# Two token-wise products inside block 2's attention: the copy out of PSUM moves from ScalarE to VectorE

## The reference, cut to what matters

```python
h = rms_norm(x, norm_g)
proj = jnp.einsum('btd,de->bte', h, w_in)
a_q, a_k, a_v, a_g, b_q, b_k, b_v, b_g, m_q, m_g = jnp.split(proj, cuts, axis=-1)
...
oa = from_heads(moba_attention(qa, ka, to_heads(a_v, 6)))       # heads "a", 6 of 64
ob = from_heads(dilated_attention(qb, kb, to_heads(b_v, 6)))    # heads "b", 6 of 64
om = from_heads(memory_attention(qm, km, to_heads(m_v, 4)))     # memory heads, 4 of 64
y = jnp.concatenate([oa * silu(a_g), ob * silu(b_g), om * silu(m_g)], axis=-1)
return x + jnp.einsum('bte,ed->btd', y, w_out)
```

## Time and profile before

| | |
|---|---|
| median of 3 runs | 1651.87 us (1651.77 to 1654.35) |
| the profiled execution's own time | 1654.05 us |
| its span | 1652.2 us |
| TensorE busy | 1583.6 us, 96% |
| VectorE busy | 912.7 us, 55% |
| ScalarE busy | 770.0 us, 47% |
| mean granted TensorE clock | 0.997 |

### The profile page before, as it was taken

How to read it: one execution, slowest core, us unless ns; L and a number is a source line. 1 busy time by engine, 2 the same in 40 slices (tenths; PEclk the granted TensorE clock), 3 DMA queues, 4 the chain that set the end, 5 groups by cost and what they waited for, 6 DMA issues and landing times.

```text
span 1652.2 us, 22035 instructions
## 1 busy us (share of the span) xinstructions
PE 1583.6 (96%) x8345; PEld 1307.0 (79%) x8345; DVE 912.7 (55%) x1924; ACT 770.0 (47%) x1599; POOL 46.7 (3%) x75
## 2 busy tenths in 40 slices
PE   6999999999999999999999999999999999989999
PEld 6887768788887887777788888898866679977667
DVE  4597546443445379546444335568664464965443
ACT  4443444333334352545333334435667553456772
POOL 0000001000001000001100000100000010000000
PEclk9999999999999999999999999999999999999999
DMA  7232112333332333112233333332212233311121
GB/s 217 87 89 77 51 39 77 92 100 90 90 106 75 98 102 90 52 52 79 65 89 102 99 92 115 99 90 69 70 37 62 75 90 96 96 45 58 40 76 64
DMA packets 80885, 136.07 MB, mean 82 GB/s; under 512 B 8190, under 2 KB 33548, under 8 KB 80780
## 3 DMA queue, kind: packets, MB, share of 16 engines
q1 hardware_dynamic: 77120, 129.22, 26.9%
q10 hardware_dynamic: 3660, 5.44, 1.2%
HBM read 132.55 MB, written 2.10 MB: 81 GB/s over the span
## 4 chain that ended last, share of the span: by engine, by line
PE 82%; DVE 8%; ACT 7%; issue 2%; DMA 0%; ACTq 0%; POOL 0%; DVEq 0%
PE gemm_bank L725 68%; PE aux_bank L851 3%; PE aux_bank L830 2%; PE aux_bank L795 2%; PE aux_bank L811 2%; ACT probs L1160 2%; PE aux_bank L780 1%; DVE w_lo L1466 1%; ACT w_hi L1104 1%; PE aux_bank L839 1%; ACT spread_inv L1174 1%; ACT probsT L1195 1%; DVE rope L1565 1%; DVE probs L1624 1%; PE aux_bank L697 1%
## 5 line engine op out<-in xcount | busy, mean ns | idle before, releaser
L1104 ACT ACTIVATE w_hi<-raw 128x512 fp32r<-128x512 f32 (+3 forms) x524 | 305.1, 587 | 640.9 <-PE gemm_bank L725 640.3
L1466 DVE TENSOR_TENSOR w_lo<-raw,w_hi 128x512 fp32r<-128x512 f32 (+3 forms) x524 | 330.1, 635 | 447.3 <-ACT w_hi L1104 446.2
L725 PE MATMUL gemm_bank<-act_hi,w_hi 128*128 128x512 f32 x768 | 311.1, 405 | 5.4 <-ACT bgT L1417 2.1
L725 PE MATMUL gemm_bank<-act_hi,w_lo 128*128 128x512 f32 x768 | 299.8, 390 | 0.0
L725 PE MATMUL gemm_bank<-act_lo,w_hi 128*128 128x512 f32 x768 | 299.5, 390 | 0.0
L725 PE MATMUL gemm_bank<-w_hi,act_hi 128*128 128x384 f32 (+3 forms) x736 | 266.0, 361 | 1.1 <-DVE qk_c L1506 1.1
L725 PE MATMUL gemm_bank<-w_hi,act_lo 128*128 128x384 f32 (+3 forms) x736 | 257.3, 350 | 0.0
L725 PE MATMUL gemm_bank<-w_lo,act_hi 128*128 128x384 f32 (+3 forms) x736 | 257.2, 349 | 0.0
L725 PEld LDWEIGHTS gemm_bank<-act_hi,w_hi 128*128 128x128 f32 x768 | 144.3, 188 | 43.3 <-issue 11.1
L725 PEld LDWEIGHTS gemm_bank<-act_hi,w_lo 128*128 128x128 f32 x768 | 144.1, 188 | 30.8
L725 PEld LDWEIGHTS gemm_bank<-act_lo,w_hi 128*128 128x128 f32 x768 | 144.5, 188 | 28.6 <-issue 1.0
(11 more groups left out here) (302 smaller groups left out, 2101.2 us busy)
## 6 DMA issues: line engine op xcount, KB each, us to landing
raw<-in_w_in SPq DMA_DIRECT2D x104, 512.0 KB, 3.6
raw<-in_w_in SPq DMA_DIRECT2D x64, 384.0 KB, 3.3
raw<-in_w_out SPq DMA_DIRECT2D x32, 512.0 KB, 3.9
raw<-in_w_branch SPq DMA_DIRECT2D x24, 512.0 KB, 3.8
raw<-in_w_mem_kv SPq DMA_DIRECT2D x8, 512.0 KB, 3.7
raw<-in_w_in SPq DMA_DIRECT2D x16, 256.0 KB, 2.8
raw<-in_w_in SPq DMA_DIRECT2D x8, 416.0 KB, 4.9
x<-in_x SPq DMA_DIRECT2D x4, 512.0 KB, 5.1
```

Of the source, the lines that this page charges most:

```text
L725: last = pe.matmul(o, a, c, start=begin and n == 0, stop=end and n == 2)
L1104: act.activation(w_hi[:, s % RING, 0:n], raw[:, p % RAW, kk % PIECE, 0:n], ACT.Copy)\
L1466: dve.tensor_tensor(w_lo[:, s % RING, 0:n], raw[:, p % RAW, kk % PIECE, 0:n], w_hi[:, s % RING, 0:n].bitcast(F32), ALU.subtract).then_inc( ...
```

## The change

Within block 2's attention, the four banks of bv and the four of mq are copied to SBUF by VectorE (tensor_copy) and not by ScalarE (activation Copy). On each engine the copies stand at the same place in the written order, in split_beside of the step in which the group ends. Sixteen instructions change their engine: four for bv and four for mq, in each of two layers. No other eviction is changed.

```diff
 def evict_beside(gi):                      # ScalarE
     name = group_key[gi][2]
     if name in gates_T:
         ...
-    elif name in ("bv", "mq"):
-        evict_now(gi, ACT.Copy, lambda b: flat_2(name)[:, b, :])
...
+def evict_tokens(gi):                      # VectorE
+    name = group_key[gi][2]
+    if name in ("bv", "mq"):
+        evict_now(gi, lambda b: flat_2(name)[:, b, :])
+
-attention(a, out_2, None, beside_steps, drain)
+attention(a, out_2, evict_tokens, beside_steps, drain)
```

## The result

| | before | changed |
|---|---|---|
| median of 8 runs each, side by side | 1653.11 us (1651.44 to 1655.39) | 1662.09 us (1657.16 to 1664.21) |
| ratio, 95% interval | | 1.0046 [1.0035, 1.0056] |
| the profiled execution's own time, span | 1654.05, 1652.2 us | 1663.78, 1662.0 us |
| mean granted clock in it | 0.997 | 0.994 |

The change makes the kernel slower: by 9.0 us between the two medians, by 7.6 us by the ratio. The direction was foreseen; the median lies 1.6 us above the range's upper end of 1660.5 us.

What follows compares the result with a forecast made beforehand. TensorE's waits were taken to bound the kernel: 2 x (2.45 - 0.42) = 4.06 us, plus one slow clock spell of 1.56 us, gave 5.62 us on 1651.87, so 1657.5 us. The range was 1653.5 to 1660.5 us.

Steps and rivals of the forecast that it cites:

- What bounds the kernel: Whole kernel: TensorE, busy 96% of the span, bounds it; only its waits count, not work moved between ScalarE and VectorE.
- ScalarE's relief is worth its full length: Rival: ScalarE's saved work in both layers counts fully, 6.2 us off, 1645.7 us; chance 0.02.
- bv, step 6: Where bv ends: VectorE's copies wait behind two b heads' pieces, so TensorE stalls 2.45 us a layer; removal from ScalarE saves nothing.
- The w_lo behind the copies at nothing: Step 6, VectorE: the w_lo delayed by bv's copies costs nothing; at most 1.95 us if its cover were gone.
- lateness spreads: Rival: VectorE's copies push w_lo or the next scores past TensorE's need, up to 3.9 us more, 1659.8 us; chance 0.06.
- mq, step 11: Where mq ends: copies fit VectorE's idle time, ScalarE's w_hi comes earlier, gaining 0.42 us a layer; L839 wait falls to 0.15.
- Not given back: After step 6: the 2.45 us stall is not recovered, as the chain has no wait for another engine until 1189.71 us.
- not slower: Rival: VectorE reaches bank 0's copy in time or a later wait swallows the delay, 1651.0 us; chance 0.10.
- The sum: Both layers: stall at bv less gain at mq, 2 x (2.45 - 0.42) = 4.06 us slower.
- The clock: Behind the new stalls: one spell at the 1.2 GHz clock in the two layers, costing 1.56 us more.

Runs made afterwards that it cites:

- bv alone: Kernel before with only bv's copies moved to VectorE, mq's left on ScalarE: 1659.75 us, ratio 1.0040.
- Copies first: Changed kernel with VectorE's copies put ahead of the two pieces of the b heads: 1652.33 us, ratio 1.0001 to before.
- values first: Changed kernel with TensorE doing the values of pair 0 between bv's last and mq's first matmul: 1651.86 us, ratio 0.9994 to before.
- the stall is filled: Changed kernel with nine useless TensorE matmuls in the step 6 wait, run twice: 1660.49 and 1659.27 us.
- mq alone: Kernel before with only mq's copies moved to VectorE, bv's left on ScalarE: 1653.43 us, ratio 1.0003.
- the longer kernels: Kernels 4 us and more longer than before: those with bv's copies behind the b heads' pieces, and before with 9, 15 or 18 useless matmuls; medians 1657.39 to 1662.09 us.

## Why the prediction was right and wrong

- **What bounds the kernel: right.** ScalarE's 5.1 us less of work brought nothing at bv. The rival by which ScalarE's relief is worth its full length falls.
- **bv, step 6: right, in mechanism and size.** 2.45 us forecast; 2.45 to 2.47 in the traces of the changed kernel and of bv alone, at the steps where no spell is mixed in. Copies first takes 1.86 us of it away by VectorE's order alone, and values first takes all but 0.05 us away by giving TensorE something else to do meanwhile.
- **The w_lo behind the copies at nothing: right.** It is 1.9 us later in VectorE's order and no wait for it appears. The rival in which lateness spreads falls.
- **mq, step 11: right in the sum, coarse in its place.** The gain is 0.42 to 0.45 us a layer against 0.42: ScalarE's w_hi, and with it spread_inv, comes that much earlier. But the wait ahead of L839 falls from 0.57 only to 0.33 us, not to 0.15, because TensorE gets there earlier too: from mq's last matmul to the transposes of the probabilities it took 1193.79 - 1192.07 = 1.72 us before and 1198.84 - 1197.33 = 1.51 us after. The matmul at 1192.33 us wants bank 0, which ScalarE began to copy only at 1191.82 us; that this was a short wait fits the times, but the trace of before gives it no row.
- **Not given back: right.** The lag moves at no other wait. The rival "not slower" falls: the copy of bank 0 starts at 1178.06 us. In time would have been 1172.95 us of before plus the lag of 2.78 us that TensorE had by then, so 1175.73 us; it is 2.3 us late.
- **The sum: right.** 4.06 us forecast, measured as 4.06 us in the first trace and 4.04 us in the third, where no spell is mixed in.
- **The clock: this step failed.** It said: "I take one spell in the two layers as the likeliest count: 4.06 + 1.56 = 5.62 us." The size of a spell was right (1.46 to 1.62 us behind the layer 1 stall), and in the four traces with an idle stall three of eight stalls had one behind them. But the term was to be the difference in time that the clock makes. The excess that should have been that term is 3.2 +-1.2 us over the 18 runs of the changed kernel (mean 1660.37 us), twice the term, and it is 2.7 +-1.4 us when the stall is filled. So "A stall of TensorE has a second price here" is not borne out. Two places of one trace, one with a spell and one without, said nothing on how many spells a kernel has on average. That trace had another spell at 1452 us, which the forecast passed over; the longest wait of TensorE in the 12 us ahead of it was 1.2 us, not 1.82:

```profile
1452.00:1454.00 2.00, 2.00 (x9) 2.00 (x10) 1.93 (x8) 0.00 (x0) 0.00 (x0) 0.50 0.00 0
```

What makes the excess instead stays open; the runs show that it goes with more time at the lower clock all over the kernel and with the slow start.

Taken literally, the Trainium skill's page "TensorE: Matmul & The Clock Gate", section "What's actually happening", gives the half clock to idle windows alone; the spells behind stalls of 2.2 us with matmuls on either side disagree, as before.

- **The rest of the miss.** The forecast stood on the median of three runs, 1651.87 us, and the eight runs beside the changed kernel had 1653.11. So of 1662.09 - 1657.5 = 4.6 us, 1.24 us is base, and the other 3.35 us is beyond the forecast sum and its one spell. With the base put right the range would end at 1661.7 us, still below the result. Over all 18 runs the changed kernel's median is 1660.2 us, just inside the range; that its first eight came out 1.9 us above that can be chance (their mean is 2.2 +-2.3 us above that of the other ten).

## What to carry to other kernels

Price a moved eviction by what stands ahead of it in its new engine's queue, against when TensorE wants the bank: here a copy takes about the same on either engine (0.49 us on ScalarE, 0.55 on VectorE), and its place in VectorE's queue cost 2.46 us a layer, of which the two 0.95 us pieces in front of it made 1.86. If the move is wanted, put the copy ahead of such pieces, which left 0.61 us, or give TensorE other work until then, which left 0.05. For effects below half a per cent, pair the matmuls of several traces and read the lag at the changed places: it repeated to 0.03 us, while the whole time moved by 1.2 to 1.6 us with each clock spell that came or went.

## What the runs showed of the hardware that was not expected

- The same kernel has its spells at other places from execution to execution: spans of 1662.0, 1655.6 and 1660.7 us, and times from 1656.8 to 1664.2 us in 18 runs. Of two equal waits of 1.8 us, one in each layer, the first has a spell behind it in one trace of the kernel before, and the second in the next.
- Spells come in two lengths: 1.2 to 1.6 us lost, and some 3.0 us (at 1267 us in the first trace of the changed kernel, at 1575 us in the third), with a clock of 0.50 for 4 to 6 us.
- A spell at 19 us is in both traces of before and missing in those of mq alone, copies first and values first, none of which changes anything there; it moves the lag by 1.2 us right at the start. In the nine traces of the longer kernels the matmuls run at the slow rate from the first one until 20 to 22 us (421 ns each, as above), which costs about the same as that spell, and the clock column doesn't show it.
